# Local attention in a two-layer encoder: values become the stationary operand, and the row sums and the norm move

## What is computed

```python
def windowed_gqa(q, k, v, sink):          # 8 heads of 64, 2 of keys and values, blocks of 128, band of 3 blocks
    ...
    m = jnp.maximum(jnp.max(s, axis=-1, keepdims=True), sink_l)
    p = jnp.exp(s - m)
    denom = jnp.sum(p, axis=-1, keepdims=True) + jnp.exp(sink_l - m)
    o = jnp.einsum('bnhgqk,bnkhd->bnqhgd', (p / denom).astype(v.dtype), vw)
    return o.reshape(B, S, ATT_WIDTH)
...
    y_att = rms_norm(windowed_gqa(aq, ak, av, sink), att_g).astype(x.dtype)
    ...
    return jnp.concatenate([y_att, y_ml], axis=-1) @ w_out
...
        x = layer_norm(ALPHA * x + y, ln1_g[l], ln1_b[l])
```

## Time and profile before

| what | value |
|---|---|
| median of 3 runs | 2233.62 us (2233.3 to 2236.38) |
| profiled execution | 2236.14 us, its span 2234.6 us |
| mean granted TensorE clock | 0.98 |
| TensorE busy | 2109.9 us, 94% |
| VectorE busy | 1330.3 us, 60% |
| ScalarE busy | 996.6 us, 45% |
| slots of layer 0 | 81.1 to 283.4 us |
| slots of layer 1 | 1164.7 to 1368.2 us |

### The profile page before, as it was taken

One profiled execution on the slowest core, in us unless ns is written; L12 is line 12 of the kernel. 1 busy time (PEld: TensorE's weight loads), 2 busy tenths in 40 slices (PEclk: granted clock), 3 DMA queues, 4 the chain that ended last, 5 costly groups with the idle time before them and its releaser, 6 DMA issues.

```text
span 2234.6 us, 31576 instructions
## 1 busy us (share of the span) xinstructions
PE 2109.9 (94%) x11392; PEld 1698.4 (76%) x11392; DVE 1330.3 (60%) x2057; ACT 996.6 (45%) x1656; POOL 227.8 (10%) x268
## 2 busy tenths in 40 slices
PE   7899999999999899999798999999999989999997
PEld 7778867888887577777577887788887867777774
DVE  3785477831454756566878646783325476665566
ACT  3554565232422354555235547533333135555553
POOL 0000023000000311000200001300000032200004
PEclk9999999999998899999899999999999999999999
DMA  4164112221102699999511112023120059999996
GB/s 153 57 198 147 39 76 96 95 94 57 57 29 100 232 369 376 385 377 347 197 58 38 39 39 95 20 115 115 74 76 10 38 215 371 372 378 377 374 383 222
DMA packets 78534, 384.88 MB, mean 172 GB/s; under 512 B 10473, under 2 KB 11865, under 8 KB 43609
## 3 DMA queue, kind: packets, MB, share of 16 engines
q1 hardware_dynamic: 55264, 327.31, 38.8%
q0 software_dynamic: 10096, 30.38, 3.9%
q10 hardware_dynamic: 13064, 25.75, 3.1%
HBM read 352.27 MB, written 46.07 MB: 178 GB/s over the span
## 4 chain that ended last, share of the span: by engine, by line
PE 73%; DVE 14%; ACT 7%; issue 2%; DMA 2%; POOL 1%; DVEq 0%; ACTq 0%; POOLq 0%; SPq 0%
PE bank L2201 30%; PE bank L2712 10%; PE bank L2686 8%; PE bank L2676 7%; PE bank L2413 5%; PE bank L2444 2%; PE bank L2523 2%; DVE weight_slots_parts L1437 2%; PE bank L2222 1%; PE bank L2652 1%; ACT scratch L1059 1%; DVE scratch L1599 1%; PE bank L2567 1%; PE bank L2583 1%; PE bank L2606 1%
## 5 line engine op out<-in xcount | busy, mean ns | idle before, releaser
L1907 DVE TENSOR_TENSOR weight_slots_parts<-weight_slots,mixer_region_parts 128x2048 fp32r<-128x2048 f32 x140 | 322.9, 2327 | 85.5 <-ACT mixer_region_parts L1261 85.4
L2201 PE MATMUL bank<-weight_slots_parts,x_transposed_parts 128*128 128x256 f32 (+1 forms) x1248 | 299.1, 334 | 7.0 <-DVE mixed L1559 4.2
L1261 ACT ACTIVATE mixer_region_parts<-weight_slots 128x2048 fp32r<-128x2048 f32 x140 | 260.9, 1909 | 23.2 <-ACT x_transposed L1336 18.1
L2201 PE MATMUL bank<-x_transposed_parts,weight_slots_parts 128*128 128x512 f32 (+1 forms) x1024 | 262.7, 343 | 6.9 <-DVE mixer_region L1551 3.7
L1437 DVE TENSOR_TENSOR weight_slots_parts<-weight_slots,weight_slots_parts 128x2048 fp32r<-128x2048 f32 x58 | 132.9, 2292 | 193.5 <-ACT weight_slots_parts L950 192.8
L2712 PE MATMUL bank<-weight_slots,x_transposed 128*128 128x512 f32 x560 | 248.0, 596 | 0.0
L2201 PEld LDWEIGHTS bank<-weight_slots_parts,x_transposed_parts 128*128 128x128 f32 x1248 | 210.7, 193 | 26.2 <-DVE mixed L1559 5.0
L2686 PE MATMUL bank<-mixer_region_parts,x_transposed_parts 128*128 128x256 f32 x1120 | 207.7, 283 | 0.7 <-DVE weight_slots_parts L1907 0.6
L2201 PEld LDWEIGHTS bank<-x_transposed_parts,weight_slots_parts 128*128 128x128 f32 x1024 | 180.0, 193 | 28.7 <-DVE mixer_region L1551 4.5
L2676 PE MATMUL bank<-mixer_region_parts,x_transposed_parts 128*128 128x512 f32 x560 | 193.9, 418 | 4.6 <-DVE x_transposed_parts L1912 4.6
L2712 PEld LDWEIGHTS bank<-weight_slots,x_transposed 128*128 128x128 f32 x560 | 104.2, 191 | 118.8 <-issue 103.2
(11 more groups left out here) (319 smaller groups left out, 3590.3 us busy)
## 6 DMA issues: line engine op xcount, KB each, us to landing
weight_slots<-in_w_gate SPq DMA_DIRECT2D x70, 1024.0 KB, 7.4
weight_slots<-in_w_up SPq DMA_DIRECT2D x70, 1024.0 KB, 7.2
weight_slots<-in_w_down SPq DMA_DIRECT2D x70, 1024.0 KB
weight_slots<-in_w_in SPq DMA_DIRECT2D x20, 1024.0 KB, 5.2
slots_y<-x_transposed ACTq DMA_DIRECT2D x66, 256.0 KB, 7.3
weight_slots<-in_wkv_mem SPq DMA_DIRECT2D x16, 1024.0 KB, 4.7
slots_y<-in_consts SPq DMA_DIRECT2D x6, 2304.0 KB, 17.0
weight_slots<-in_w_out SPq DMA_DIRECT2D x8, 1024.0 KB, 4.8
```

Source lines behind the costliest of these rows:

```text
L1261: nc.scalar.activation(hi, raw, ACT.Copy).then_inc(moe.high_ready, 1)
L1907: v.tensor_tensor(lo, raw, hi.bitcast(F32), ALU.subtract).then_inc(moe.low_ready, 1)
L2201: ins = pe.matmul(ps, lhs[i](k), rhs[j](k), start=k == 0 and a == 0, stop=k == KD - 1 and a == 2)
```

## The change

The product of probabilities and values is exchanged: 64 columns of values are now the weights and the probabilities of the two heads that share them (256 columns) stream through, so the output stands turned, head dimension down and tokens across. The two key/value heads write PSUM partitions 0 to 63 and 64 to 127. It follows that:

- the division by the sums must come before the product: VectorE multiplies `probs` in place (`normalise`), and TensorE's turns wait for that;
- the turned probabilities are packed in full banks, two or three tiles of 512 columns in place of four;
- ScalarE, not VectorE, copies `pv` to `y`;
- nothing has to be turned for the output product; `high_y` and `low_y_attention` split straight from `y`;
- the sum of squares runs across partitions: ScalarE squares, VectorE adds four (`sum_squares`), TensorE multiplies with a column of ones (`sum_tokens`), ScalarE makes the factor, and VectorE applies it with the residual (`attention_half`); ALPHA is applied in `add_half`;
- the norm's gain goes into weight units wo0 and wo1, whose two splits become four pieces each.

```diff
-            for j in range(GRP):
-                add(("pt", i - 1, j), (4, 5))
+            for b in range(keys_of(GROUP_ORDER[i - 1][0])[1]):
+                add(("pt", i - 1, b), (4, 5))
...
+    add(("rs", 0), (4, 5))
...
-                for c in YT_BEHIND[s] if g == 0 else ():
-                    add(("yt", c, 0), (4, 5, 6, 7))
+            if g == 0:
+                add(("rs", 1), (7,))
...
+                            for j in range(GRP - 1):
+                                nc.scalar.activation(hi[:, j, :], raw[:, j, :], ACT.Copy, scale=lane_gain[:, j:j + 1])
...
+                            for b in range(keys_of(GROUP_ORDER[i - 1][0])[1]):
+                                drain_copy(("pt", i - 1, b), ptb[:, 512 * b:512 * b + 512], 512)
...
                             nc.scalar.activation(st[:, 12:16], st[:, 12:16], ACT.Exp).then_inc(p_ready, 1)
                             own(p_ready)
+                        if i:
+                            c, jp = GROUP_ORDER[i - 1]
+                            drain_copy(("pv", i - 1), y[:, c, 256 * jp:256 * jp + 256], 256)
...
+                            for j in range(GRP):
+                                ins = v.scalar_tensor_tensor(out=lo[:, j, :], in0=raw[:, j, :], scalar=lane_gain[:, j:j + 1], in1=hi[:, j, :],
+                                                             op0=ALU.mult, op1=ALU.subtract)
...
+                    def sum_squares(c):
+                        dve.wait_ge(turned, len(TURNED) * now[0] + TURNED[("squares", c)] + 1)
+                        sq = qT[:, :, c * P:(c + 1) * P] if c < NC - 1 else esc[:, :].rearrange("p (j t) -> p j t", j=GRP)
+                        v.tensor_reduce(sums_at(c), sq.rearrange("p j t -> p t j"), AX.X, ALU.add).then_inc(att_parts, 1)
+                        own(att_parts)
+
+                    def normalise(i):
+                        nk = keys_of(GROUP_ORDER[i][0])[1] * P
+                        dve.wait_ge(p_ready, 12 * l + i + 1)
+                        step(v.tensor_tensor(st[:, 110:114], st[:, 8:12], st[:, 12:16], ALU.add))
+                        step(v.reciprocal(st[:, 110:114], st[:, 110:114]))
+                        for j in range(GRP):
+                            ins = v.tensor_scalar(probs[:, j, 0:nk], probs[:, j, 0:nk], st[:, 110 + j:111 + j], None, ALU.mult)
+                        ins.then_inc(p_scaled, 1)
+                        own(p_scaled)
...
                         if w and i:
                             stream_tile(w[0])
...
+                        if i < 12:
+                            normalise(i)
+                        if i >= 8:
+                            sum_squares(i - 8)
                         for t in w[1:]:
                             stream_tile(t)
...
-                            pe.wait_ge(p_ready, 12 * l + i)
-                            for j in range(GRP):
-                                turn_probs(j)
+                            pe.wait_ge(p_scaled, 12 * l + i)
+                            turn_probs()
...
-                            for t in range(GRP):
-                                n, _ = head_at(jp, t)
-                                for k in range(nb):
-                                    ins = pe.matmul(ps[:, t * HD:(t + 1) * HD], ptb[:, t, k * P:(k + 1) * P],
-                                                    kv[:, k0 + k, NKV * HD + n * HD:NKV * HD + (n + 1) * HD],
+                            for k in range(nb):
+                                for n in range(NKV):
+                                    out = ps[n * HD:(n + 1) * HD, 0:2 * P].rearrange("p (j q) -> p j q", j=2)
+                                    mine = ptb[:, 0:GRP * nb * P].rearrange("p (j n k q) -> p n k j q", j=2, n=NKV, k=nb)[:, n, k, :, :]
+                                    ins = pe.matmul(out, kv[:, k0 + k, NKV * HD + n * HD:NKV * HD + (n + 1) * HD], mine,
                                                     start=(k == 0), stop=(k == nb - 1))
```

178 lines of the change are left out of this document (104 added, 74 removed).

## The result

The changed kernel took 2278.65 us (median of four runs, 2275.51 to 2284.01) beside 2234.28 us for the kernel before: ratio 1.0209, 95% interval 1.019 to 1.0227. Measured a second time beside other runs, it came out at 2272.59 us and 1.0162 (1.0146 to 1.0178). The forecast was 2259 us with a range up to 2271: the sign was right and the size was not. The loss forecast as 24 us was 44 us by the medians and 39 us by the profiled executions (2273.9 against 2234.6 us).

A forecast was written before the change was run, and what follows sets the result against it. VectorE and ScalarE's loop was taken to bound slots 0 to 5, TensorE mostly from slot 7. Terms of +12.7 us in layer 0 and +11.0 in layer 1 gave +23.7, stated as 2259 us, range 2231 to 2271.

The forecast's parts named there:

- I take these to cancel: -0.2: Behind the slots: fewer turns, added one-column products, ScalarE's later decay chain and its shorter factor nearly cancel, -0.2 us per layer.
- +0.6: Behind the slots: wo1's split in pieces adds 0.8 us on VectorE, where TensorE waits at times; +0.6 us per layer.
- +6.7 us in layer 0, +5.0 in layer 1: Start of slot 7: later by VectorE's longer loop, less its former waits for TensorE, plus 0.4 us in slot 6.
- A stretch of 3.9 in slot 6 I leave out: Slot 6: a 3.9 us TensorE idle stretch, at the edge of lowering the clock, given no clock cost.
- -0.8 each: Slots 7 and 8: TensorE saves 1.2 us, of which 0.8 is left after ScalarE's added copy; -1.6 us per layer.
- no overlap at all: Product in two-key-block slots: stays at 1.89 us, TensorE loses some 0.3 us per slot, the sum rises about 5 us.
- `sum_squares` +0.65: Slots 9 and 11: VectorE's strided sum of 512 columns delays emptying the gate tile's bank by 0.65 us.
- the same shift meets a bank that is free some 0.9 early: +0.4: Slot 10: slot 9's shift of +1.3 us is partly absorbed by an early free bank, leaving +0.4 us.
- 4.4 and 5.0: Slots 9 and 11: TensorE idle for a gate tile's bank, in us, each followed by 1.5 us of lower clock.
- The mask of group 11 begins near 5.2: Slot 11: VectorE's mask starts near 5.2 us into the slot, not 3.7, after wo0's split in four pieces.
- B: Rival: TensorE decides everywhere because the multiplications run under VectorE's existing waits; a gain, about 2219 us, chance 0.13.
- D: Rival: column halves do not overlap, and slots 3 to 6 also fall to the lower clock; 2276 us, chance 0.07.

The follow-up runs named there:

- the version with the lows moved: Changed kernel with the four moves, the product's copy behind the first stream tile in slots 1 to 6, and VectorE's wo1 low parts behind group 1's token tiles: 2224.55 us, 0.9966.
- the moves: Changed kernel with division before the finish, sums of squares late, ScalarE's product copy and squares late, token sums in banks 5 and 6: 2230.89 us, 0.9988.

## Why the forecast was right in sign and short in size

**Which step failed.** The forecast had 23.7 us and the profiled executions 39.3. Nearly half of the 15.6 us between them, 7.4, lie behind the slots, where the forecast wrote "I take these to cancel: -0.2" and "+0.6" and summed to +0.4 per layer: this is the step that failed, since two waits and a lower clock there had no term. Slot 10, forecast "+0.4", is 3.3 more over both layers, and slots 0 to 6 are 3.0 more; the rest is terms of under 2 us each way and scatter.

**Slots 0 to 6, "+6.7 us in layer 0, +5.0 in layer 1".** Measured 7.1 and 7.6 (the terms as written add up to 6.8 and 5.3). Slots 0 to 5 took 6.2 and 5.2 us more, where the forecast's terms give 6.4 and 4.9, so the sum of durations along VectorE's loop held: behind the finish, most of what is added is paid for. Slot 2 took 14.74 us from mask to mask (118.03 to 132.77) where 14.3 was forecast, and the wait at the turns of slot 3, forecast as 6 us, was 4.65. What missed its term is slot 6, +0.8 and +2.4 against +0.4. TensorE waited 3.37 us there in both layers; the granted clock over the next 4 us was 1.00 in layer 0 and 0.64 in layer 1, and the forecast had left that stretch out ("A stretch of 3.9 in slot 6 I leave out"). That the sum came so near is in part luck: the second measurement has +11.1 and +6.2, so no more than the mean of the four, 8.0, is firm. What the forecast did not ask is whether the same operations would be nearly free elsewhere: moved ahead of the finish, they gave back as much as leaving out the multiplications.

**Slots 7 and 8, "-0.8 each".** Measured -0.47 each. TensorE's own gain was 1.31, near the 1.2 forecast (packing 0.73, product 0.58 from start to start). The other case that the forecast named, no overlap at all and a loss of 0.3 us a slot, whose 0.3 no row supports, is thereby ruled out. ScalarE took 0.85 of it where 0.4 was allowed: mask, exponentials, copy (0.39), square (0.63) and the `v` tile's emptying make a chain of 15.64 us. ScalarE squared in this place before too, but TensorE's own 16.10 us covered it.

**Slots 9 to 11.** The term "`sum_squares` +0.65" measured 1.02 to 1.09. The term of slot 10, "the same shift meets a bank that is free some 0.9 early: +0.4", was mis-sized, and its clock was left out. With the clock held (layer 1) it measured +1.3. The reader of the bank began 14.0 us into the slot of layer 0 and 12.0 before, 2.0 later and not 1.3, for the sum was longer and the mask began only 0.5 us sooner, not 1.0. TensorE waited 2.31 us there in both layers. In layer 0 the tile behind the wait took 4.39 us at a granted clock of 0.65, such as the forecast gave to slots 9 and 11 alone; in layer 1 the same wait was followed by 1.00:

```profile
273.50:277.90 4.40, 4.40 (x26) 4.27 (x26) 1.46 (x4) 4.18 (x8) 0.00 (x0) 0.65 0.00 0
1370.20:1373.30 3.10, 3.06 (x24) 2.94 (x24) 1.28 (x3) 2.87 (x6) 0.00 (x0) 1.00 0.00 0
```

The first is layer 0, the second layer 1; hence +2.8 and +1.3. The waits in slots 9 and 11 were forecast as 4.4 and 5.0 and measured 4.67 and, in slot 11, 3.69 in layer 0 and 4.76 in layer 1. "The mask of group 11 begins near 5.2" us into its slot was 3.6 in layer 0, where slot 10 was drawn out by the clock, and 5.0 in layer 1; the low pieces of wo0 measured 2.74, not 3.1.

**Behind the slots, "I take these to cancel: -0.2" and "+0.6" for wo1.** Measured +2.8 and +5.4 from the first mLSTM scores, and here causes were missing altogether. The low parts of wo1 took 4.56 us, not 3.1, since GpSimd works beside them; at the place that is 1.9 to 2.1 us a layer. The token sums' banks are those of the first early tiles, emptied by ScalarE behind its chain: 3.84 us of wait, worth 1.8 to 2.1. The plan of banks was in the code and was not read for this. With both mended the stage took 127.2 and 127.4 us, 1.0 less than before the change in layer 0 and 1.3 more in layer 1. The third is the clock. Over the first 26 us of the stage, in layers 0 and 1 of the kernel before, then of the version with the lows moved:

```profile
286.00:312.00 26.00, 22.45 (x111) 16.15 (x110) 18.96 (x47) 18.02 (x34) 5.13 (x15) 0.93 0.31 127
1370.70:1396.70 26.00, 22.45 (x116) 15.78 (x115) 20.30 (x49) 19.52 (x37) 6.02 (x18) 1.00 0.31 126
```

```profile
282.30:308.30 26.00, 22.00 (x89) 14.86 (x89) 17.98 (x44) 20.25 (x40) 5.03 (x16) 0.87 0.26 107
1357.20:1383.20 26.00, 22.02 (x89) 14.97 (x89) 17.82 (x44) 20.14 (x40) 4.99 (x16) 0.87 0.27 109
```

In the changed kernel too it is 0.87 in both layers, so the step down is larger in layer 1, where more was lost. That fits the 1.3 us left over and the difference between the layers, but no run changes the clock alone, so its price here is not shown.

**The rivals.** B (TensorE decides, 2219) named the condition rightly: it holds once VectorE's addition hides under its waits. In the order as written it doesn't. With the moves it does in most slots, and the measured 2224.55 is near that number, in part by luck: it also has the other banks and the later low parts, which B did not count, and it still loses clock behind the slots. D asked for halves that do not overlap, which is refuted. The range ended at 2271 since D had 0.07; its second half, lower clock in more slots, is part of what happened.

## What to carry to other kernels

Price an added step by what stands ahead of it in its engine's queue before pricing its duration: the same multiplications cost 7.6 to 9.1 us a layer behind a wait and 1.0 to 1.6 inside it. When a change hands a bank from one engine to another, list all that the new owner does ahead of emptying it, and for each new tile who has the same bank next. And try the parts of a change singly: the packing gained 6 us in a kernel that lost 39.
